# A two-layer encoder trunk on one core: x loaded with its axes turned, and the first weights' low part moved to GpSimd

## The reference, cut to what matters

```python
def reference(x, positions, w_in, ...):
    for l in range(DEPTH):
        proj = x @ w_in[l]                       # 1024 columns in, 2208 out
        q_lat, kv_lat, k_rope, sc_b, sc_c, sc_h, cf_a, cf_g, gq_q, gq_k, gq_v = split(proj)
        y_a = mla_attention(...)                 # dense attention
        y_b = sc_b * depthwise_conv(sc_c * sc_h, sconv_w[l])
        y_c = conformer_conv(cf_a, cf_g, cconv_w[l], ...)   # 31 taps
        y_d = window_gqa(...)                    # banded attention
        mix = concat(y_a, y_b, y_c, y_d) @ w_out[l]
        x = layer_norm(ALPHA * x + mix)
        x = layer_norm(ALPHA * x + expert_choice_moe(x, ...))   # 16 experts
```

## Time and profile before

| | |
|---|---|
| median of 3 runs | 1472.83 us (1471.87 to 1474.85) |
| the profiled execution's own time | 1471.98 us |
| its span, first to last instruction | 1470.2 us |
| busy PE / DVE / ACT / POOL | 1365.1 / 496.2 / 293.1 / 105.8 us |
| mean granted TensorE clock | 0.988 |

### The profile page before, as it was taken

One profiled execution on the slowest core, in us unless ns is written; L12 is line 12 of the kernel. 1 busy time (PEld: TensorE's weight loads), 2 busy tenths in 40 slices (PEclk: granted clock), 3 DMA queues, 4 the chain that ended last, 5 costly groups with the idle time before them and its releaser, 6 DMA issues.

```text
span 1470.2 us, 15583 instructions
## 1 busy us (share of the span) xinstructions
PE 1365.1 (93%) x6372; PEld 711.5 (48%) x6372; DVE 496.2 (34%) x1001; ACT 293.1 (20%) x517; POOL 105.8 (7%) x86
## 2 busy tenths in 40 slices
PE   6999999899999999989889998999999999999894
PEld 5766578444334334333467575774343343343332
DVE  6775745311111111110549467261201201201205
ACT  4236630010001001000043457111100000000000
POOL 2320000000000000000133200000000000000001
PEclk9999999999999999999999999999999999999997
DMA  9100353999999999999950012469999999999993
GB/s 377 70 1 1 144 202 150 381 429 416 427 427 429 427 427 427 426 428 427 421 232 0 0 58 100 193 255 388 429 414 428 428 428 427 427 425 429 427 427 163
DMA packets 44405, 459.94 MB, mean 313 GB/s; under 512 B 7856, under 2 KB 8624, under 8 KB 14640
## 3 DMA queue, kind: packets, MB, share of 16 engines
q1 hardware_dynamic: 34416, 436.88, 70.8%
q10 hardware_dynamic: 6752, 10.54, 2.0%
q0 software_dynamic: 3168, 11.54, 1.9%
HBM read 450.55 MB, written 8.39 MB: 312 GB/s over the span
## 4 chain that ended last, share of the span: by engine, by line
PE 75%; DMA 12%; DVE 5%; issue 3%; ACT 3%; ACTq 1%; SPq 0%; DVEq 0%; POOLq 0%
PE bank L914 24%; PE bank L937 13%; PE bank L534 11%; DMA ring<-w_moe 10%; PE bank L881 8%; PE bank L791 2%; PE bank L795 2%; PE bank L794 2%; DMA wr<-w_router 2%; PE bank L489 2%; PE bank L852 1%; PE bank L679 1%; PE bank L959 1%; PE bank L869 1%; PE bank L567 1%
## 5 line engine op out<-in xcount | busy, mean ns | idle before, releaser
L914 PE MATMUL bank<-ring,work 128*64 128x512 f32 x1632 | 357.3, 594 | 13.0 <-issue 8.8
L914 PEld LDWEIGHTS bank<-ring,work 128*64 128x64 f32 x1632 | 134.0, 137 | 222.0 <-issue 201.1
L937 PE MATMUL bank<-ring,w_up 128*64 128x512 f32 x800 | 180.4, 600 | 14.5 <-ACT w_up L1834 9.3
L1512 DVE TENSOR_TENSOR work<-work,bank 128x512 f32<-128x512 f32 x32 | 22.0, 688 | 473.1 <-PE bank L914 472.3
L1531 DVE TENSOR_TENSOR X<-X,bank 128x512 f32<-128x512 f32 x112 | 77.1, 688 | 251.4 <-PE bank L881 251.4
L881 PE MATMUL bank<-work,cst 128*128 128x512 f32 x240 | 116.3, 618 | 9.7 <-ACT work L1855 9.7
L937 PEld LDWEIGHTS bank<-ring,w_up 128*64 128x64 f32 x800 | 63.0, 138 | 121.7 <-issue 106.2
L914 PE MATMUL bank<-work 128*64 128x512 f32 x416 | 92.4, 593 | 1.5 <-issue 1.5
L534 PE MATMUL bank<-x_hi,w_hi 128*128 128x512 f32 x288 | 79.2, 420 | 7.8 <-ACT w_hi L1602 4.1
L881 PEld LDWEIGHTS bank<-work,cst 128*128 128x128 f32 x240 | 38.6, 189 | 87.3 <-DVE X L1531 36.7
L1151 DVE SCALAR_TENSOR_TENSOR bank<-X,par,bank 128x512 f32<-128x512 f32 x120 | 79.9, 748 | 0.9 <-DVE ring L1125 0.9
(11 more groups left out here) (225 smaller groups left out, 1513.7 us busy)
## 6 DMA issues: line engine op xcount, KB each, us to landing
ring<-w_moe SPq DMA_DIRECT2D x146, 2048.0 KB, 25.5
work<-w_moe SPq DMA_DIRECT2D x36, 2048.0 KB, 21.2
ring<-w_moe SPq DMA_DIRECT2D x20, 1024.0 KB, 8.4
ring<-w_in SPq DMA_DIRECT2D x18, 1024.0 KB, 15.7
ring<-w_out SPq DMA_DIRECT2D x8, 1024.0 KB, 29.7
work<-ln SPq DMA_DIRECT2D x4, 1024.0 KB, 16.8
x_rows<-X ACTq DMA_DIRECT2D x8, 512.0 KB, 6.1
out<-X POOLq DMA_DIRECT2D x8, 512.0 KB, 6.5
```

The costliest lines, as they stand in the source:

```text
L914: ins = mm(B((kind, pair, n))[64 * e:64 * e + 64, :], xsT[:, k, 64 * e:64 * e + 64], w[:, e, n * 512:(n + 1) * 512], start=(k == 0), stop= ...
L937: ins = mm(B(("O", pair, n))[64 * e:64 * e + 64, :], hidT[:, k, 64 * e:64 * e + 64], w[:, i, e], start=(k == 0), stop=(k == KD - 1))
L1512: nc.vector.tensor_tensor(hid[:, cols], hid[:, cols], B(("U", pair, n))[:, :], ALU.mult)\
```

## The change: what it does

The host hands in x a second time as `x_turned`, 128 partitions x 8 blocks x 512 rows. In the first layer SyncE loads it in four parts of two blocks each into `XT`, which lies over the space of `X`; the load of the first weights is issued between parts 1 and 2. TensorE turns nothing in this layer and only marks the eight "xT" names as full. ScalarE makes `x_hi` block by block from `XT`, with the first weights' high part ahead of block 4 and behind the wait for part 2. VectorE makes `x_lo` block by block from `XT` and frees the "xT" names in the order of k. In the very first projection TensorE waits for `x_hi` block by block rather than for all of it. The first weights' low part is made by GpSimd instead of VectorE, ahead of its own seven. The second layer is as it was.

```diff
+        XT = view(Xf, 0, KD, S)
...
             sp.dma_start(cst[:, 0:ONES], consts[:, 0:ONES]).then_inc(ident_in, 16)
-            for t in TILE_ORDER:
-                sp.dma_start(X[:, t], x_in[t * P:(t + 1) * P]).then_inc(x_in_tile[t], 16)
+            for g in range(NT):
+                if g == 2:
+                    sp.dma_start(ring[:, 0], w_in[0, 0]).then_inc(slot_full[0], 16)
+                sp.dma_start(XT[:, 2 * g:2 * g + 2], x_turned[:, 2 * g:2 * g + 2]).then_inc(x_in_part[g], 16)
...
                 for place, t in enumerate(TILE_ORDER):
-                    if lay == 0:
-                        pe.wait_ge(x_in_tile[t], 16)
                     for half in range(2):
+                        if lay == 0:
+                            pe.sem_inc(fullsem(("xT", t, half)), 1)
+                            continue
...
                         for k in range(KD):
+                            if lay + i == 0 and (w, x) == HI_HI:
+                                pe.wait_ge(x_hi_ready, k + 1)
...
-                pe.wait_ge(x_hi_ready, at(lay, 2 * NT, 2 * NT))
+                if lay > 0:
+                    pe.wait_ge(x_hi_ready, at(lay, 2 * NT, 2 * NT))
...
                 if lay == 0:
                     angles()
-
-                for place in (2, 0, 1, 3):
+                    for k in range(KD):
+                        name = ("xT", TILE_ORDER[k // 2], k % 2)
+                        full(v, name, lay)
+                        v.wait_ge(x_hi_ready, k + 1)
+                        nc.vector.tensor_tensor(x_lo[:, k], XT[:, k], x_hi[:, k].bitcast(F32), ALU.subtract)\
+                            .then_inc(freesem(name), 1)
+
+                for place in (2, 0, 1, 3) if lay > 0 else ():
...
-                v.wait_ge(w_hi_ready, at(lay, IN_SLOTS, 1))
-                nc.vector.tensor_tensor(w_lo[0], ring[:, 0], w_hi[:, 0].bitcast(F32), ALU.subtract)\
-                    .then_inc(w_lo0_ready, 1)
+                if lay > 0:
+                    v.wait_ge(w_hi_ready, at(lay, IN_SLOTS, 1))
+                    nc.vector.tensor_tensor(w_lo[0], ring[:, 0], w_hi[:, 0].bitcast(F32), ALU.subtract)\
+                        .then_inc(w_lo0_ready, 1)
...
-                for place, t in enumerate(TILE_ORDER):
-                    if lay > 0 and place == 2:
+                for k in range(KD if lay == 0 else 0):
+                    ac.wait_ge(x_in_part[k // 2], 16)
+                    if k == 4:
+                        w_high(0)
+                    act(x_hi[:, k], XT[:, k], ACT.Copy).then_inc(x_hi_ready, 1)
+                for place, t in enumerate(TILE_ORDER if lay > 0 else ()):
+                    if place == 2:
                         w_high(0)
...
                 if lay == 0:
-                    w_high(0)
                     ac.wait_ge(angles_ready, 1)
...
+                if lay == 0:
+                    hold(w_hi_ready, 1)
+                    tt(w_lo[0], ring[:, 0], w_hi[:, 0].bitcast(F32), ALU.subtract).then_inc(w_lo0_ready, 1)
                 for n in range(1, IN_SLOTS - 1):
                     w_low(n)
```

More of the change, by code:

```diff
@@ L203, with trunk @@
 USES, PER_LAYER = bank_uses()
-def trunk(nc, x_in, positions, tokens, w_in, w_uq, w_ukv, w_router, params, w_out, ln1, ln2, w_moe,
+def trunk(nc, x_in, x_turned, positions, tokens, w_in, w_uq, w_ukv, w_router, params, w_out, ln1, ln2, w_moe,
           consts, iota, out):
@@ L350, in trunk @@
         ident_in, consts_in, iota_in, pos_in = sem("ident_in"), sem("consts_in"), sem("iota_in"), sem("pos_in")
-        x_in_tile = [sem(f"x_in{t}") for t in range(NT)]
+        x_in_part = [sem(f"x_in{g}") for g in range(NT)]
         params_in, ln1_in, ln2_in = sem("params_in"), sem("ln1_in"), sem("ln2_in")
@@ L449, in _ @@
                 for kind, n in LOADS:
+                    if (lay, kind, n) == (0, "w", 0):
+                        continue
                     slot, _ = LOADED[kind, n]
@@ L2007, in lay_out @@
     return {
-        "x_in": a["x"].reshape(S, D), "positions": a["positions"].reshape(S), "tokens": tokens, "w_in": w_in, "w_uq": uq,
+        "x_in": a["x"].reshape(S, D), "x_turned": a["x"].reshape(S, KD, P).transpose(2, 1, 0), "positions": a["positions"].reshape(S), "tokens": tokens, "w_in": w_in, "w_uq": uq,
         "w_ukv": ukv, "w_router": a["w_router"], "params": par, "w_out": w_out,
```

## The result

| | before | after |
|---|---|---|
| median of 6 runs each | 1473.86 us | 1478.69 us (1476.12 to 1479.74) |
| ratio of the runs, 95% interval | | 1.0037 (1.0026 to 1.0047) |
| span of the profiled execution | 1470.2 us | 1476.8 us |

The ratio's interval is 3.8 to 6.9 us. The forecast was 1479.0 us and +6.2; the medians differ by 4.8, the two profiled spans by 6.6. Five microseconds in 1474 are little, but they arise in one place, and the trace shows it.

A forecast was written before the change was run, and what follows sets the result against it. In the head the chain was bound by w_router's landing at 46.02 us, then VectorE; from 60.88 by TensorE. TensorE 7.9 us late, less 1.7 of waiting, gives +6.2: 1479.0 us, range 1475.0 to 1482.5.

The forecast's parts named there:

- Loads and ScalarE: Head of the first layer: x part 0 lands at 7.3 us; the first weights' high part runs 12.4 to 14.3.
- Who holds TensorE back: First projection: TensorE waits for VectorE's x_lo, banks 0 and 1 coming free only as blocks 4 and 5.
- The first collision: GpSimd's operation on the first weights, until 19.5 us, holds up VectorE's angles, which are ready at 20.4.
- third rival: Angles are not held up, but x_lo is blocked until 19.15: TensorE 8.8 us late, +7.1, 1479.9; chance 18%.
- The second collision: GpSimd's operation on the second weights gets in after x_lo block 4, holding 23.5 to 28.1; blocks 5 to 7 end 30.0.
- second rival: VectorE keeps the port while its queue is full: TensorE 5.4 us late, +3.7, 1476.5; chance 14%.
- main case: GpSimd holds up VectorE's angles, then x_lo after block 4: +6.2 us, 1479.0; chance 45%.
- TensorE's sum: First projection starts at 23.5, bank 1's eight end at 28.8, all ends at 38.8: next projection 7.9 us late.
- What is swallowed: TensorE's 1.71 us wait at 60.88 absorbs part; w_router lands 46.0 to 49.0, before the convolution at 50.6, worth nothing.
- The time: Whole kernel: 7.9 - 1.7 = +6.2 us, on the 1472.83 us median shown, gives 1479.0 us.
- first rival: Nothing collides, SBUF inputs don't matter: TensorE 0.7 us late, swallowed by the 1.71 wait, 1472.8; chance 8%.

The follow-up runs named there:

- e1_hold: Changed kernel with one wait more: GpSimd begins the first weights' low part only when all x_lo blocks are done; 1472.75 us, ratio 1.0000.
- e3_order: Changed kernel with VectorE's x_lo blocks in the order 4, 5, 0, 1, 2, 3, 6, 7; 1477.91 us, ratio 1.0030.
- e2_dve_low: Changed kernel with its GpSimd part undone: VectorE makes the first weights' low part again, behind x_lo; 1472.73 us, ratio 0.9991.
- g1_late: Changed kernel with four semaphore increments delaying GpSimd's operation on the second weights in the first layer; 1475.69 us, ratio 1.0016.
- e4_pool_alone: Kernel before with only the first weights' low part moved to GpSimd in the first layer; 1474.00 us, ratio 1.0010.
- f1_free: Changed kernel: GpSimd waits until x_lo is done, VectorE takes blocks 4 and 5 first, parameter loads issued behind x_hi block 3; 1469.75 us, ratio 0.9974.
- f0_before_params: Kernel before with the four parameter loads issued ahead of the first weights' high part on ScalarE's queue; 1473.54 us, ratio 1.0001.
- h3_split: Changed kernel: low part on VectorE, GpSimd behind it, early parameter loads, 28 extra matmuls, cosine's angles after the low part, second high part before cosine; 1466.37 us, ratio 0.9955.

## Why the prediction was right, step by step

**Loads and ScalarE.** Right within 0.4 us: weights' high part at 12.01 (12.4 said), first block of x_hi at 6.97 (7.3).

**Who holds TensorE back.** Right: both its first waits are for VectorE's x_lo, by banks 0 and 1; the waits for x_hi block by block never held it. e1_hold and e3_order confirm it from two sides.

**The first collision.** Right in kind. The TENSOR_SCALAR with one SBUF input took 4.62 us beside GpSimd, which no row of before had shown. So the third rival, that the angles are not held up, is out. The Trainium skill (SBUF — State Buffer, "SBUF: two separate sides") has two-port modes excluded as well as two-input operations; this trace agrees, 4.62 us against 0.43. Mis-sized: GpSimd did not wait for L1026 to end at 14.9 but was through at 18.92 (4.73 us from 14.19), so x_lo began at 19.59, not 20.4. Nearly half of these 0.8 us come from VectorE's angles, which ran 0.36 us earlier than in the rows of before (the last group of L1026 from 12.42 instead of 12.78).

**The second collision.** The outcome was as forecast, the reason given for it was not sound, and so this was luck. I had read from L1888 that GpSimd gets in at the next boundary between VectorE's operations. Its subtraction of 128x2048 does not: in e2_dve_low and g1_late it stood across two boundaries, until VectorE's queue was empty. The small L1888 (128x1) did get in, in the kernel before: it was through at 731.65, while VectorE's second operation ran to 731.90 and the next was queued right behind it:

```profile
731.81 1.41 DVE L1053 SCALAR_TENSOR_TENSOR X<-X,stat,work 128x512 f32<-128x512 f32 x2
```

So the row was read rightly but was no guide to the large operation; why the two differ is not shown. The second rival (VectorE keeps the port, +3.7 us) was what the large one does in both of those runs. Between going first and standing lay 0.06 us of timing (0.46 and 0.52 us into a block), which the forecast could not have known. g1_late, which is that rival made real, is at +3.8 us at the rotary matmuls. So the honest weight of main case and second rival was nearer to even than 45 to 14.

**TensorE's sum.** In 2 was 7.83 us late, 7.9 said, out of three errors that cancel, and that is luck too: it began 0.7 us earlier than said, it waited 1.15 us for bank 1 instead of 1.8, and its 48 matmuls cost 3.9 us over the 10.9 of the upper clock (15.95 from 22.78 to 38.73, less the 1.15 wait), where I had 2.6 (38.8 - 23.5 - 1.8 - 10.9). The second eight, after the wait, took 3.78 us like the first: the short work before had brought no rise.

**What is swallowed.** The 1.71 us wait went as said. `w_router` landed at 44.65, earlier than my lower bound of 46.0; the convolution started with its input at 50.60 (50.6 said), so that was worth nothing.

**The time.** 1479.0 was the 1472.83 of three runs plus 6.2. On 1473.86, the median of six, the same step gives 1480.1, and the medians differ by 4.8, not 6.2. So the step of the forecast is less close than its end, though it is inside the 3.8 to 6.9 us of the ratio.

**The first rival,** nothing collides, is what e1_hold measures: 1.0000, as worked out there (0.7 late at in 2; measured 1.1).

## What to carry to other kernels

Before an elementwise operation is moved to GpSimd, or an operand of VectorE's from PSUM to SBUF, list what VectorE does in SBUF in those microseconds: here two edits, each harmless alone (e4_pool_alone, e2_dve_low), cost 5 us together. When two queues meet within a few tenths of a microsecond, put a wait there rather than trust the order; one line (e1_hold) undid the loss. And an earlier stage pays only once the next hold in the chain has moved too: f1_free gained when the collision, the bank order and the parameter loads were changed together, where none of them alone got below the kernel before (e1_hold, e3_order, f0_before_params). The early parameter loads alone, at 9.78 us, were not run.

## What the runs showed of the hardware that was not expected

- A GpSimd subtraction of 128x2048 that stands behind VectorE's queued two-input operations stands until the last of them is done: 7.42 us instead of 4.6 in e2_dve_low, 6.14 in g1_late. In the changed kernel and in e3_order it went first, and the VectorE operation took 5.03 and 5.05 us instead of 0.68. A single VectorE operation does the same: in f0_before_params VectorE's low part began 0.22 us ahead of GpSimd's and took 2.28 us, and GpSimd's took 6.53; in the kernel before, GpSimd began 0.24 us ahead, took 4.58, and VectorE's took 6.50.
- Where VectorE's operations wait for each other, with 0.03 to 0.04 us between them, it gets in: in h3_split it asked at 21.44, 0.17 us into the second of three (21.27), took 4.98 us, and VectorE's second and third together took 5.70 us instead of 1.4. At the same 0.17 us into a queued block, in g1_late, it stood.
- STREAM_SHUFFLE (SBUF to SBUF) and operations with a PSUM input run beside GpSimd undisturbed: 0.73 us and 4.87 us for eight.
- The landing of a load of 64-byte rows, 64 KB in all, took 29.9 to 31.2 us from its issue in the five runs that issued it at 9.7 to 9.8 us, with the big loads under way; issued at 15.2 us it took 31.0, at 19.5 us 26.5, at 21.8 us 22.9.
- TensorE's first 16 matmuls of the projection, where it had done nothing before them, took 5.25 to 6.72 us (six runs); behind 34 extra matmuls they took 3.90.
- TensorE's clock: in the changed kernel eight matmuls took 3.75 us (0.47 each, the lower level) while the granted clock is shown as 1.00, as the window shows (us, busy of PE, PEld, DVE, ACT, POOL, granted clock, DMA share, GB/s):

```profile
22.00:27.00 5.00, 3.75 (x8) 2.48 (x8) 5.00 (x3) 1.56 (x2) 4.54 (x1) 1.00 1.02 414
```

Until the first change of level in a run the column doesn't tell the level; the matmuls' own pace does.
